# Gate groups of the first stage: six instead of three, four of them summed in SBUF

## What is computed

```python
ada = silu(c) @ w_ada + b_ada                      # 6 x 2048 conditioning values, 9 columns
h   = rmsnorm(x, g_norm1) * (1 + sc1) + sh1        # needs the first third of ada
... gate_gdn, gate_dsa = split(h @ w_in)           # 2 x 2048 gate features, among others
o_gdn = gated_delta_rule(...)                      # recurrence in chunks
o_dsa = sparse_attention(...)
mix = sigmoid(gate_gdn) * (o_gdn @ w_gdn_out) + sigmoid(gate_dsa) * (o_dsa @ w_dsa_out)
x   = x + gt1 * (mix @ w_o)                        # then the feed-forward half
```

## Time and profile before

| | us |
|---|---|
| median of 3 runs | 1920.74 |
| span of the profiled execution | 1917.2 |
| PE busy (matmul) | 1863.7 |
| PE weight loads busy | 1753.1 |
| GpSimd busy | 1185.7 |
| ScalarE busy | 806.5 |
| VectorE busy | 626.6 |

### The profile page before, as it was taken

The page is one execution under the profiler, slowest core; times in us unless marked ns, Lnnn a source line. Parts: engine busy times, 40 slices in busy tenths (PEclk is TensorE's granted clock), DMA queues, the critical chain, the costliest instruction groups (busy, mean ns, idle before and its releaser), DMA issues.

```text
span 1917.2 us, 41636 instructions
## 1 busy us (share of the span) xinstructions
PE 1863.7 (97%) x16742; PEld 1753.1 (91%) x16742; DVE 626.6 (33%) x1791; ACT 806.5 (42%) x1353; POOL 1185.7 (62%) x508
## 2 busy tenths in 40 slices
PE   6989999999999999999999999999999999999997
PEld 2689999999888878888999899999999999999996
DVE  3224654444423242322442433220132231123333
ACT  3354445665323222323434655543344443344442
POOL 0267666666444334436877677777777777777773
PEclk9999999999999999999999999999999999999998
DMA  9966544444687878789764454555555555545552
GB/s 392 405 261 217 178 149 134 148 148 143 227 296 250 307 241 295 239 290 298 229 237 159 154 166 165 166 167 166 167 165 164 164 164 166 166 166 167 167 184 83
DMA packets 145102, 390.69 MB, mean 204 GB/s; under 512 B 27522, under 2 KB 36162, under 8 KB 144322
## 3 DMA queue, kind: packets, MB, share of 16 engines
q1 hardware_dynamic: 124976, 374.01, 57.6%
q10 hardware_dynamic: 19986, 14.70, 2.5%
HBM read 379.70 MB, written 8.88 MB: 203 GB/s over the span
## 4 chain that ended last, share of the span: by engine, by line
PE 91%; DMA 4%; DVE 2%; issue 1%; ACT 1%; POOL 1%; DVEq 0%; SPq 0%; ACTq 0%; POOLq 0%; PEldq 0%
PE bank L2391 27%; PE bank L2392 26%; PE bank L2396 26%; PE bank L2351 3%; DMA raw_a<-in_stream 2%; DMA raw_c<-in_stream 1%; PE bank L2887 1%; PE bank L2340 1%; PE bank L2325 1%; PE bank L2476 0%; PE bank L2772 0%; POOL rest_a L822 0%; PE bank L2622 0%; PE bank L2756 0%; DVE x L2315 0%
## 5 line engine op out<-in xcount | busy, mean ns | idle before, releaser
L822 POOL TENSOR_TENSOR rest_a<-raw_a,hi_a 128x1024 fp32r<-128x1024 f32 x168 | 402.2, 2395 | 241.2 <-ACT hi_a L882 241.2
L2391 PE MATMUL bank<-h_hi,hi_a 128*128 128x288 f32 x1720 | 475.9, 303 | 3.0 <-ACT hi_a L882 1.8
L2392 PE MATMUL bank<-h_lo,hi_a 128*128 128x288 f32 x1720 | 465.6, 296 | 0.0
L2391 PEld LDWEIGHTS bank<-h_hi,hi_a 128*128 128x128 f32 x1720 | 325.5, 189 | 21.3 <-issue 15.6
L2392 PEld LDWEIGHTS bank<-h_lo,hi_a 128*128 128x128 f32 x1720 | 326.2, 190 | 0.4
L882 ACT ACTIVATE hi_a<-raw_a 128x1024 fp32r<-128x1024 f32 x168 | 177.8, 1060 | 289.9 <-PE bank L2396 219.8
L822 POOL TENSOR_TENSOR rest_b<-raw_b,hi_a 128x1024 fp32r<-128x1024 f32 x74 | 177.9, 2404 | 103.2 <-ACT hi_a L882 103.2
L2396 PE MATMUL bank<-h_hi,rest_a 128*128 128x288 f32 x1488 | 226.7, 294 | 1.3 <-POOL rest_a L822 1.3
L2396 PEld LDWEIGHTS bank<-h_hi,rest_a 128*128 128x128 f32 x1488 | 207.1, 188 | 1.6 <-POOL rest_a L822 1.6
L2391 PE MATMUL bank<-h_hi,hi_b 128*128 128x288 f32 x648 | 176.8, 299 | 0.0
L2392 PE MATMUL bank<-h_lo,hi_b 128*128 128x288 f32 x648 | 174.3, 295 | 0.0
(11 more groups left out here) (533 smaller groups left out, 3766.8 us busy)
## 6 DMA issues: line engine op xcount, KB each, us to landing
raw_a<-in_stream SPq DMA_DIRECT2D x364, 512.0 KB, 3.6
raw_b<-in_stream SPq DMA_DIRECT2D x179, 512.0 KB, 3.5
raw_c<-in_stream SPq DMA_DIRECT2D x94, 512.0 KB, 3.4
raw_m<-in_stream SPq DMA_DIRECT2D x27, 512.0 KB, 6.5
raw_e<-in_stream SPq DMA_DIRECT2D x12, 512.0 KB, 10.0
st<-in_state ACTq DMA_DIRECT2D x8, 512.0 KB, 6.1
st<-in_state SPq DMA_DIRECT2D x8, 512.0 KB, 6.5
out_state_s<-st ACTq DMA_DIRECT2D x8, 512.0 KB, 6.1
```

The lines of the kernel that those rows point to most:

```text
L822: nc.gpsimd.tensor_tensor(rest_in(name, r), raw_of(name, r), w_hi[q].bitcast(f32), ALU.subtract).then_inc(lo_ready, 1)
L2391: MM(banks[c][:, 0:N], w_, hi_of(k), start=(first and k == 0), stop=False)
L2392: ins = MM(banks[c][:, 0:N], w_, lo_of(k), start=False, stop=False)
```

## The change

- Six gate groups (0 to 5) are made early, 24 slots. They run by quarters: all six groups' slots of quarter 0, then of quarter 1, and so on. Sixteen stand in PE's loop, from (5, 2) on, one more, then the last turn, then seven.
- Groups 0 and 1 are held in banks 0 to 3 as before (`N_HELD`). The slots of groups 2 to 5 (`TURNS_OF`) use banks 6 and 7, each quarter for itself, and VectorE copies or adds it to `park` in SBUF (`evict`). The next such slot waits for that. The last one but one uses banks 4 and 5.
- Loads stand 6 places ahead in 4 raw buffers; 18 of them stand ahead of the last conditioning slot.
- The four squares' sums are made in n = 1 and the sums on PE behind slot (2, 1); the function table for Ln is loaded before the squares (`early_ln`); the squares wait for one half of x each; the scalings are in n = 3 and 4.
- Twelve sigmoids instead of six in `early_gates`. The mix stage has 56 D slots instead of 68; `FILL` is new, with runs of three A slots. Some scratch tiles are elsewhere.

```diff
-N_EARLY = 3
-EARLY = [(e % N_EARLY, e // N_EARLY) for e in range(N_EARLY * (KT // KS))]
-EARLY_AT = {(7, 0): (0,), (8, 0): (1,), (9, 0): (2,), (10, 0): (3,), (11, 0): (4,), (12, 0): (5,), (14, 0): (6,), (15, 4): (7, 8)}
+N_EARLY, N_HELD = 6, 2
+QUARTER = ((2, 0, 3, 1, 4, 5), (2, 0, 3, 1, 4, 5), (2, 3, 0, 4, 1, 5), (0, 2, 1, 3, 5, 4))
+EARLY = [(g, s_) for s_, order in enumerate(QUARTER) for g in order]
+TURNS_OF = [e for e, (g, _) in enumerate(EARLY) if g >= N_HELD]
+EARLY_AT = {(5, 2): (0,), (6, 0): (1,), (6, 2): (2,), (7, 0): (3,), (7, 2): (4,), (8, 1): (5,),
+            (9, 0): (6,), (9, 2): (7,), (10, 1): (8,), (11, 0): (9,), (11, 2): (10,), (12, 1): (11,),
+            (13, 0): (12,), (13, 2): (13,), (14, 1): (14,), (15, 1): (15,), (15, 4): (16, 17)}
-LEAD, RAW_E = 4, 3
+LEAD, RAW_E = 6, 4
...
-FILL = ("DAADAADAADAAD" + "DAADAADAADAA") * (NA // 16) + "DAADAADAADAAD"
+FILL = (2 * "DAADAADAADAA" + "DAAADAAADAA") * (NA // 24) + "D"
...
+            act.wait_ge(const_in, 48)
+            early_ln()
             for q in range(4):
                 square_quad(q)
-            act.wait_ge(const_in, 48)
             rms(0)
...
+            def evict(e):
+
+                g, s_ = EARLY[e]
+                dve.wait_ge(early_done, e + 1)
+                for c in range(CT):
+                    to, of = park[CT * g + c], bank[early_bank(e) + c][:, 0:N]
+                    last = CP(to, of) if s_ == 0 else T_(to, to, of, ALU.add)
+                last.then_inc(evicted, 1)
+
             for n in range(2 * KT // CT):
                 if n >= 1:
                     cond_copy(n - 1)
                     if n == 1:
                         dve.wait_ge(const_in, 48)
+                    if n == 9:
+                        evict(6)
+                    if n == 13:
+                        evict(12)
                     cond_bias(n - 1)
...
+                if n == 1:
+                    for q in range(4):
+                        add_squares(q)
+                if n == 3:
+                    dve.wait_ge(rs_ready, 1)
+                    scale_x(0)
+                    scale_x(1)
+                if n == 4:
+                    scale_x(2)
+                    samples(0)
+                    scale_x(3)
                     lo_pair(0)
-                if n == 6:
                     lo_pair(1)
                     lo_samples(0)
...
+                if n == 5:
+                    evict(0)
+                if n == 6:
+                    evict(2)
+                if n == 7:
+                    evict(4)
+                if n == 8:
+                    evict(5)
+                if n == 10:
+                    evict(8)
+                if n == 11:
+                    evict(10)
+                if n == 12:
+                    evict(11)
+                if n == 13:
+                    evict(13)
+                if n == 15:
+                    evict(15)
...
+            for e in (17, 19, 21, 22, 23):
+                evict(e)
...
-                if (g, s_) == (2, 0):
+                held = g < N_HELD
+                if e == 0:
                     pe.wait_ge(xr_ready, 4)
+                elif early_bank(e) == 6:
+                    pe.wait_ge(evicted, sum(e_ < e for e_ in TURNS_OF if early_bank(e_) == 6))
+                elif early_bank(e) == 4:
+                    pe.wait_ge(bias_done, 2 * KT // CT)
...
-                    if s_ == 3 and n in (2, 3):
-                        first_sum(2 * n - 4)
-                        first_sum(2 * n - 3)
+                    if (n, s_) == (2, 1):
+                        for q in range(4):
+                            first_sum(q)
```

More of the change, by code:

```diff
@@ L461, in decoder_step @@
         sq_ = Place(rest_at + 4 * CT * N_EARLY * N)
-        sqp_k = sq_.take("sqp_k", [P, H, SEQ])
+        sqp_k = Place(dead_at).take("sqp_k", [P, H, SEQ])
         sqs = sq_.take("sqs", [P, 2 * H, NS])
@@ L473, in decoder_step @@
         assert gq.at >= tp.at
-        park_a = Place(gq.at).take("park_a", [P, CT * N_EARLY - 1, N])
-        park = [park_a[:, t, :] for t in range(CT * N_EARLY - 1)] + [qkv[:, QKV_T - 4, :]]
-        assert gq.at + 4 * (CT * N_EARLY - 1) * N <= nc.sbuf_usable_end
+        park_a = Place(gq.at).take("park_a", [P, 5, N])
+        park = [park_a[:, t, :] for t in range(5)] + [qkv[:, t, :] for t in range(QKV_T - 5, QKV_T)] \
+            + [ada[:, 2 * (q + 1) * KT:2 * (q + 2) * KT, :].rearrange("p k n -> p (k n)") for q in range(2)]
+        assert len(park) == CT * N_EARLY and jp.at <= qkv_at + 4 * (QKV_T - 5) * N
+        assert gq.at + 4 * 5 * N <= nc.sbuf_usable_end
         st_p = gq.take("st_p", [P, 2, P])
@@ L737, in _ @@
                         if what in (("ada1", 2), ("ada1", 4)):
-                            k0, done = (0 if what[1] == 2 else KT // 2), x_in
+                            k0, done = (0, x_back[0]) if what[1] == 2 else (KT // 2, x_back[1])
                             sp.dma_start(x[:, k0:k0 + KT // 2, :].rearrange("p k n -> p (k n)"),
@@ L938, in keep_early @@
             def keep_early(g):
-                act.wait_ge(early_done, len(EARLY) - N_EARLY + g + 1)
+                e = EARLY.index((g, KT // KS - 1))
+                act.wait_ge(early_done, e + 1)
                 for c in range(CT):
-                    last = A_(park[CT * g + c], bank[E_BANK[g] + c][:, 0:N], ACT.Copy)
+                    last = A_(park[CT * g + c], bank[early_bank(e) + c][:, 0:N], ACT.Copy)
                 last.then_inc(parked, 1)
@@ L947, in early_gates @@
                 act.wait_ge(X["o"], UNITS)
+                act.wait_ge(evicted, len(TURNS_OF))
                 for g in range(N_EARLY):
@@ L959, in _ @@
             round_samples(0)
-            hi("early", 0)
+            for e in range(4):
+                hi("early", e)
             round_pair(2)
-            hi("early", 1)
-            hi("early", 2)
+            for e in range(4, 8):
+                hi("early", e)
             round_pair(3)
             round_samples(1)
-            hi("early", 3)
+            for e in range(8, 11):
+                hi("early", e)
             round_pair(4)
-            hi("early", 4)
-            hi("early", 5)
+            for e in range(11, 14):
+                hi("early", e)
             round_pair(5)
             round_samples(2)
-            hi("early", 6)
+            for e in range(14, 17):
+                hi("early", e)
             round_pair(6)
-            for e in (7, 8, 9):
+            for e in range(17, 20):
                 hi("early", e)
@@ L977, in _ @@
             round_samples(3)
-            hi("early", 10)
-            hi("early", 11)
-            for g in range(N_EARLY):
+            hi("early", 20)
+            hi("early", 21)
+            keep_early(0)
+            hi("early", 22)
+            hi("early", 23)
+            keep_early(1)
+            for g in range(3):
                 hi("in", g)
-                keep_early(g)
             def hi_in(j):
@@ L2472, in rotate @@
                 pe.wait_ge(X["raw"], m + 1)
+                pe.wait_ge(evicted, len(TURNS_OF))
                 if m:
```

40 lines of the change are left out of this document (18 added, 22 removed).

## The result

The changed kernel takes 1945.91 us (median of 4 runs, 1942.53 to 1949.29) against 1920.09 us for the kernel before beside it (1916.5 to 1923.35): ratio 1.0135, 95% interval 1.0118 to 1.0152. It is 25.8 us slower; the prediction was 1922.7 us, range 1915 to 1930, with 0.25 on slower. The profiled execution spans 1940.7 us, 23.5 more than before.

The account below looks back on a forecast made before the run. The first stage was taken as bound by the weight stream and nearly by PE, everything later by PE. Span 1917.2 - 7.2 (moved work) + 1.0 (sigmoids) + 8.2 (mix) = 1919.2, median 3.5 over: 1922.7 us, range 1915 to 1930.

Parts of the forecast that it names:

- early slot 0: First stage: early slot 0 behind conditioning slot 21 starts at 43.7 us, set by the weight stream, not the root.
- the interleaved part: First stage, 16 early slots among 10.5 conditioning groups: 79.3 us plus evictions and clock, ending at 126.7.
- the end of the stage: First stage after the interleaved slots: remaining early slots, turn and a 1.1 us wait, ending at 154.1 us.
- the sigmoids: Stage ahead of the mix: six more sigmoids on ScalarE delay a weight rounding, PE waits +1.0 us, ends 0 and 2.1.
- the mix: Mix stage: 38.2 us less PE work, but +8.2 us of waits and half clock from less filler.
- Edits that cost nothing: Stream total, SP's gated early loads, moved sigmoids and scratch tiles: no cost; up to 2 us if the gate's cover goes.
- Rival 3: First stage: VectorE's row of scalings, samples and roundings delays early slot 0 to 46, +2 us, 1925; chance 0.05.
- Evictions: First stage: copies and adds of bank pairs to SBUF delay turn copies, 3 us in all, ends 0 and 14.
- The clock in the first stage: Ahead of early slot 0: a half-clock stretch behind PE's wait for the stream costs 0.7 us, ends 0 and 1.7.
- The rule weighed: Mix stage: by the skill page's weight-load share, a sixth isn't bound by slots, so twelve slots save 32 us.
- Rival 2: Mix stage: the weight stream binds, D slots come late by 1 us at five or six places, 1928; chance 0.25.
- Rival 1: Whole kernel: the gain arrives because waits in mix and first stage are smaller, -5.5 us or better, 1915; chance 0.27.

Follow-up runs that it names:

- e_order: Changed kernel with ScalarE's first roundings of early weights moved so GpSimd's subtractions don't run beside VectorE's first low parts: 1946.1 us.
- e_best: e_three with large mix slots placed one gap forward at two places, and the last pair and samples rounded ahead of early weights 18 and 19: 1910.9 us.
- e_root: e_best with PE's sums for the first root back at their old places, behind slots (2, 3) and (3, 3): 1915.9 us.
- e_rawe6: Changed kernel with six buffers for early loads instead of four: 1936.8 us, ratio 1.0056 to 1.0117 to the kernel before.
- e_three: Changed kernel with the edits of e_rawe6, e_order and e_go together: 1926.1 us.
- e_warm: e_three with three extra matmuls behind conditioning slots ahead of early slot 0, to keep PE's clock up: 1931.4 us.
- e_go: Changed kernel with the weight buffers of the stage behind the mix taken from buffer 1 on, not 0: 1940.4 us.
- e_noln: e_three without the early logarithm on ScalarE: 1930.5 us, one run.

## Why the prediction was wrong, point by point

The 21.5 us by which the span missed are, in the prediction's terms: early slot 0 +4.5, the interleaved part +7.8, the end of the stage -0.3, the sigmoids -1.0, the mix +4.9, and +5.6 behind the mix, where it had no term. The step that failed most is the one that put the gated loads under "Edits that cost nothing".

*Early slot 0* (43.7 predicted, 48.2 seen). "The stream sets this start, not the root" left out VectorE's own row of work. Without the standstill beside GpSimd it is 45.1 (e_order, e_best). The 1.4 us left are about what PE's half clock costs there: in e_best slot 20, a turn and slot 21 take 3.1 us from 42.0, and at full clock the same three take 1.5 (an estimate from the kernel before, 87.26 to 88.80). Rival 3 named the row, at 46, and not its cause. That the sooner root allows the start is right, and worth 3.3 us (e_root).

*The gated loads* (nothing, up to 2; 6.0 seen in e_rawe6 against after, 7.1 in e_three against e_order, 8.4 in the interleaved part alone). "SP's early loads wait for slot e - 4" was applied to the end of the stage, where it hides, and not to its start, where SP stands 20.1 us at load 4 (32.7 to 52.9) with the conditioning loads behind it.

*The interleaved part.* 79.3 + 3 + 0.7 = 83.0 us predicted from early slot 0 to slot 16, 90.8 seen (48.2 to 139.0), 82.4 once the stream runs (e_three, 45.0 to 127.4). That 83.0 comes so near is luck in part: the 3 us for evictions weren't there, and the half clock under early slot 0 costs 1.9, not 0.7 (e_warm, at full clock, takes 80.6). The prices of a slot and a group, 79.3 in all, were short by the 1.3 us that remain.

*Evictions* (3 us, ends 0 and 14). Each copy or sum takes 0.45 us, as the earlier trace rows had it, and from 48.2 to 139 us PE waits for raw weights alone. With six buffers it waits for nothing from 47.6 to 130 us, the evictions included. They cost about nothing there.

*The clock in the first stage* (0.7). PE was at half clock for 17.1 us from 33.8; e_warm shows that the part ahead of the early slots is free. The two later stretches, of 3.4 us each, followed raw waits and went with them (e_rawe6).

*The end of the stage.* 27.4 us predicted for the last eight slots, 27.1 seen (139.0 to 166.1). Right, with some luck: most repaired kernels took 30.

*Twelve sigmoids* (+1.0): the stage takes 369.5 us, as before. Nothing. The six more were hidden, and PE has no wait near 484 us.

*The mix* (-30.0, seen -25.1). The waits for bt_s were predicted at 4.4 and 4.8 us and are 4.22 and 4.31: right, mechanism and size. Mis-sized were "other places, +0.4" and the clock, +1.7. Idle time rose by 10.5 us instead of 6.5, half-clocked time by 10.3 us; 2.7 of that fell into waits, and half of the rest, 3.8, is lost. Without both PE's work is 39.4 us less, against 38.2 predicted. In e_best, which has no half clock in the mix, it is 39.8 less in length with 1.8 us more of waits and 3.4 less lost to the clock: 38.2. The price by start-to-start times held.

*The rule weighed.* From what the Trainium skill (Perfetto Trace Analysis, Identifying the Most-Contended Engine) says of matmul busy time and weight loads, the prediction estimated 32 us for the twelve slots. The work that left the mix is 38.2 to 40.0 us in all kernels with the change, and e_best's mix is 39.8 us shorter: the trace doesn't agree with taking a sixth off.

*Behind the mix* (0, seen +5.6). The prediction had no term for it. It counted slots and not what 176 leaves when divided by seven buffers: the last slot, number 175 = 25 x 7, sits in buffer 0, where the next stage begins; of 188 slots the last sat in buffer 5 (e_go).

*The rivals.* Rival 2, the stream binding the mix, falls: its DMA share stayed at 0.82 and the first wait traced to raw weights is at its very end. Rival 1's gain exists, in e_best. The kernel was slower mostly for reasons that no rival held, the gate and the buffer; the one term that stood for the gate had its upper end at 2. That the forecast leaned to slower, by 2 us, is no credit to it: the two largest losses weren't in it.

## What to carry to other kernels

When transfers wait in one queue for buffers, look at what stands behind the first gated one, not the last: it holds back the whole stream until the first consumer is done. When the number of slots in a stage changes, work out anew which buffer the next stage begins with. And filler is worth what its place makes it: give the longest dependent wait its large slot first, and look again afterwards for the wait that comes next.

## What the runs showed of the hardware that was not expected

- A VectorE step of 0.18 us took 1.28, 2.07 and, for low parts of 0.28, 2.42 us beside a GpSimd subtraction of 2.35 to 2.4 us, and in two of these places it ended within 0.05 us of it. Steps reading a bank were not held up. The kernel before had it too: its amul at 46.17 us took 1.84 beside a subtraction from 45.63 to 47.98.
- PE waits of 4.2 to 5.1 us in the mix had stretches at 1.2 GHz behind them, of 3.4 or 6.8 us each. In e_best, where no wait in the mix is over 2.1 us, there is none in its 363 us. But length alone doesn't decide: in the changed kernel a wait of 1.38 at 834.4 had a stretch of 3.4 behind it and one of 1.69 at 737.3 had none.
- A stretch of 13.7 us at 1.2 GHz cost nothing where the weight stream ran at a share of 1.0 (e_warm).
- ScalarE's table load ran ahead of the wait of the instruction that needed it where nothing else stood between (18.8 us in e_noln, with the logarithm at 28.8). In the kernel before, where ScalarE's wait for the constants stood between, it came at 33.60, behind the wait for PE's sums.
